# A two-block network on one core: 352 dense tokens for 384, and five stretches re-arranged

## The chip, the core and the metric

The kernel runs on one core of a Trainium2 chip. PE (TensorE) multiplies matrices, DVE (VectorE), ACT (ScalarE) and POOL (GpSimd) work on tiles, SP issues loads. The metric is the device time of one execution in microseconds (us); the lower, the better.

## What is computed

512 tokens of width 1024 pass two blocks. The first mixes them (a state-space scan and long convolutions, the "hyena" part), adds the result and applies PEER, a layer of 16384 experts:

```python
def block(hb):                                   # 128 tokens
    q = (hb @ wq).reshape(128, 8, 2, 128)
    s = einsum('thsd,snd->thsn', q, subkeys)
    s1, i1 = top_k(s[:, :, 0], 16); s2, i2 = top_k(s[:, :, 1], 16)
    cand = (s1[..., :, None] + s2[..., None, :]).reshape(128, 8, 256)
    sc, ci = top_k(cand, 16)
    idx = e1 * 128 + e2                          # from i1, i2 at ci
    gate = softmax(sc)
    act = gelu(einsum('td,thkd->thk', hb, u_tab[idx])) * gate
    return einsum('thk,thkd->td', act, v_tab[idx])
```

The second block has two layers of SwiGLU, mixers and layer norms (`x = layer_norm(alpha * x + 0.5 * ffn(x))` and the like). All is in float32.

## The kernel before

The whole program is one list of instructions for each engine, written out in Python; semaphores (`S.on`, `S.at`) tie the engines. Nothing is scheduled by a planner: the order on an engine is the order of the calls. Functions end in the engine's letter (`_t` PE, `_v` DVE, `_a` ACT, `_g` POOL, `_s` SP).

A weight block of 128 x 1024 (a "unit") is loaded by SP into one of three staging buffers, ACT rounds it to a high half (L236), and DVE or POOL subtracts to get the low half (L242; `lo_of` says which). Three pairs of halves are held. `group` (L273 to L275) makes each product from three matmuls, high by high, high by low, low by high.

PEER treats the tokens in two ways. The last NT = 384 tokens are "dense": for each of 128 chunks of 128 experts, 8 x 3 matmuls of 128 x 384 give the products with the u table ("early"), ACT's gelu follows, the result ("act") is stored to memory, multiplied later with a dense gate table, split into halves, and 128 further units of 24 matmuls ("vexp") multiply it with the v table. The first 128 tokens, one to a partition, are served by gathers: POOL issues an indirect DMA (L2047) that fetches 128 rows of 4 KB, one for each token, into one of six row buffers; 128 gathers of u rows, each multiplied and summed by DVE (L2061), then 128 of v rows, each scaled and added by DVE (L2072). A gather waits until the row six before is used. `L.steps` spreads the rows over the stages.

The stages, in order: A, the top-k search (DVE) beside 76 early chunks; B, the gates, built by DVE as one-hot tiles (L2364: one comparison; L2366: eight small ones with the gate multiplied in) and by PE's small matmuls (L2337) for four tokens at each of 96 steps, beside 38 early chunks; C, the last 14 early chunks, where ACT begins to load acts and gates back; V, 128 units of v. In A and B POOL makes the low halves of u, in V DVE makes those of v (L242) and POOL those of the acts (L292).

Ahead of PEER stand the conv stage (L832 starts a cumulative sum in PSUM banks 4 and 5), the states stage (L603 multiplies out three "modulation" rows, all in bank 6), and the long convolutions, whose filters PE makes (L1579) and DVE multiplies with a decay out of PSUM (L1597). Behind it, `back_t` ends each part of the second block: eight groups of PE, then a layer norm (L378 POOL, L405, L412, L428 PE).

## Time and profile before

| | us |
|---|---|
| median of 3 runs | 4386.53 (4385.96 to 4389.57) |
| the profiled execution | 4381.67 |
| its span | 4379.9 |
| PE busy | 4206.7 (96%) |
| DVE, ACT, POOL busy | 2993.5, 1805.0, 1425.4 |
| stages A, B, C, V | 334, 241, 61, 533 |

Busy time says how full an engine is over the whole span, and the stages differ: what a change in a stage is worth is read from the stage's own row. PE's granted clock over the execution is 0.975.

### The profile page before, as it was taken

Reading aid. Unit: us, or ns where it says so; the run is one execution under the profiler, and the core shown is the slowest. Engines: PE = TensorE matmul, PEld = TensorE weight load, DVE = VectorE, ACT = ScalarE, POOL = GpSimd, SP = SyncE. Lnnn points to the kernel's source line nnn. Section 1 sums busy time; section 2 is a strip of 40 time slices with the busy share of each in tenths; the row PEclk is TensorE's granted clock in tenths of the full one; section 3 lists DMA queues with packets and bytes.
Section 4 is the critical chain, followed back from the end, with each engine's and each line's share of the span. In section 5 each row is a group of like instructions: output and inputs, shape, how many; then the busy total and the mean of one; then the engine's idle time right before and its main releaser. Section 6 shows DMA issues by size and latency. Waiting matters only on the chain.

```text
span 4379.9 us, 66702 instructions
## 1 busy us (share of the span) xinstructions
PE 4206.7 (96%) x26175; PEld 3683.5 (84%) x26175; DVE 2993.5 (68%) x5043; ACT 1805.0 (41%) x2815; POOL 1425.4 (33%) x992
## 2 busy tenths in 40 slices
PE   7989999999999999999999999999999999999998
PEld 5756755779999999999999877799889877877997
DVE  5866667559768977777688455498388445555873
ACT  4345411233335643333355345355255333324542
POOL 2044224315886545766411210212111110112121
PEclk9989999999999999999999999899999999899999
DMA  5123521224887899999733222123323332002332
GB/s 188 63 92 127 185 69 58 90 90 149 281 267 283 332 369 364 368 373 373 263 97 106 92 79 72 61 92 97 99 92 101 101 104 92 26 36 68 107 97 77
DMA packets 232191, 665.76 MB, mean 152 GB/s; under 512 B 22519, under 2 KB 88455, under 8 KB 229704
## 3 DMA queue, kind: packets, MB, share of 16 engines
q1 hardware_dynamic: 110528, 389.87, 26.6%
...
q14 instruction: 102, 0.84, 0.1%
HBM read 593.25 MB, written 68.16 MB: 151 GB/s over the span
## 4 chain that ended last, share of the span: by engine, by line
PE 81%; DVE 10%; issue 3%; ACT 3%; POOL 2%; DMA 1%; ACTq 0%; DVEq 0%; POOLq 0%
PE ps L273 15%; PE ps L275 15%; PE ps L274 15%; PE ps L2743 5%; PE ps L2745 5%; PE ps L2744 5%; PE ps L1624 2%; PE ps L2337 2%; PE ps L3778 1%; PE ps L1703 1%; DVE A L912 1%; DVE r L292 1%; DVE r L242 1%; DMA A<-in_w_late 1%; PE ps L405 1%
## 5 line engine op out<-in xcount | busy, mean ns | idle before, releaser
L273 PE MATMUL ps<-r,r 128*128 128x384 f32 (+1 forms) x3944 | 1435.8, 364 | 14.8 <-POOL r L242 7.2
L274 PE MATMUL ps<-r,r 128*128 128x384 f32 (+1 forms) x3944 | 1418.8, 360 | 0.0
L275 PE MATMUL ps<-r,r 128*128 128x384 f32 (+1 forms) x3944 | 1418.3, 360 | 0.0
L236 ACT ACTIVATE r<-A 128x1024 fp32r<-128x1024 f32 x513 | 542.0, 1058 | 1132.7 <-PE ps L275 996.8
L242 DVE TENSOR_TENSOR r<-A,r 128x1024 fp32r<-128x1024 f32 x401 | 509.0, 1271 | 728.2 <-ACT r L236 715.9
L273 PEld LDWEIGHTS ps<-r,r 128*128 128x128 f32 x3944 | 743.0, 188 | 101.0 <-issue 13.6
L274 PEld LDWEIGHTS ps<-r,r 128*128 128x128 f32 x3944 | 743.0, 188 | 74.6 <-issue 3.6
L275 PEld LDWEIGHTS ps<-r,r 128*128 128x128 f32 x3944 | 742.2, 188 | 74.1
L289 ACT ACTIVATE r<-A 128x512 fp32r<-128x512 f32 (+1 forms) x796 | 474.1, 611 | 497.9 <-DVE A L2429 227.9
L2743 PE MATMUL ps<-r,r 128*128 128x256 f32 x2128 | 603.0, 283 | 3.4 <-DVE A L2907 2.6
L2744 PE MATMUL ps<-r,r 128*128 128x256 f32 x2128 | 602.2, 283 | 0.0
L2745 PE MATMUL ps<-r,r 128*128 128x256 f32 x2128 | 602.2, 283 | 0.0
L292 POOL TENSOR_TENSOR r<-A,r 128x384 fp32r<-128x384 f32 (+2 forms) x243 | 338.7, 1401 | 605.3 <-ACT r L289 472.6
L292 DVE TENSOR_TENSOR r<-A,r 128x512 fp32r<-128x512 f32 x617 | 449.1, 743 | 8.2 <-ACT r L289 4.4
L2743 PEld LDWEIGHTS ps<-r,r 128*128 128x128 f32 x2128 | 408.5, 192 | 5.2 <-DVE A L2907 3.4
L2744 PEld LDWEIGHTS ps<-r,r 128*128 128x128 f32 x2128 | 408.5, 192 | 0.2
L2745 PEld LDWEIGHTS ps<-r,r 128*128 128x128 f32 x2128 | 408.5, 192 | 0.0
L242 POOL TENSOR_TENSOR r<-A,r 128x1024 fp32r<-128x1024 f32 x112 | 284.2, 2539 | 231.7 <-ACT r L236 230.4
L2925 POOL TENSOR_TENSOR A<-A 128x512 f32<-128x512 f32 x72 | 121.2, 1683 | 696.9 <-DVE A L2916 696.9
L2995 DVE TENSOR_TENSOR A<-A 128x512 f32<-128x512 f32 x304 | 208.5, 686 | 3.1 <-issue 0.2
L2072 DVE SCALAR_TENSOR_TENSOR A<-A 128x1024 f32<-128x1024 f32 x127 | 173.6, 1367 | 2.1
L2047 POOL DMA_INDIRECT A<-in_v_rows,A x128 | 160.8, 1256 | 22.0 <-DVE r L242 5.8
...
## 6 DMA issues: line engine op xcount, KB each, us to landing
A<-in_pu SPq DMA_DIRECT2D x128, 512.0 KB
A<-in_pv SPq DMA_DIRECT2D x128, 512.0 KB
...
acts<-A ACTq DMA_DIRECT2D x128, 192.0 KB
...
```

The costliest lines, as they stand in the source:

```text
L236: a.activation(self.vr(self.wr0 + 2048 * (u % RW), 1024), self.v(self.st0 + 1024 * (u % RS), 1024), ACT.Copy).then_inc(*self.S.on("a", "hi ...
L242: e.tensor_tensor(self.vr(at + 1024, 1024), self.v(self.st0 + 1024 * (u % RS), 1024), self.vr(at, 1024).bitcast(F32), ALU.subtract).then_i ...
L273: t.matmul(o, hi, xh, start=first and k == k0, stop=False)
L274: t.matmul(o, hi, xl, start=False, stop=False)
L275: m = t.matmul(o, lo, xh, start=False, stop=final and k == K - 1)
L289: a.activation(self.vr(at, n), src, ACT.Copy).then_inc(*self.S.on("a", *key))
L292: e.tensor_tensor(self.vr(lo, n), src, self.vr(at, n).bitcast(F32), ALU.subtract).then_inc(*self.S.on(who, *key))
L2072: v.scalar_tensor_tensor(out=acc, in0=row, scalar=w, in1=acc, op0=ALU.mult, op1=ALU.add).then_inc(*S.on("v", "row used", n))
L2743: t.matmul(ps[:, 0:256], hi, xh, start=opens and k == 0, stop=False, skip_group_check=not opens)
L2744: t.matmul(ps[:, 0:256], hi, xl, start=False, stop=False, skip_group_check=not opens)
L2745: m = t.matmul(ps[:, 0:256], lo, xh, start=False, stop=k == 3, skip_group_check=not opens)
L2995: v.tensor_tensor(self.operand(i, p, x), self.v(one, 512), self.v(two, 512), how).then_inc(*S.on("v", "sum", i, p, x))
```

## The change

Five things are done together.

1. NT goes from 384 to 352. The 32 tokens more (NG = 160 now) are gathered too: 160 gathers of u rows and 160 of v. Gathers n of 128 to 159 hold 32 tokens times four choices in their 128 partitions; PE copies those tokens' x four times ("x again"), four small DMAs move their indices and gates ("moved"), a second accumulator takes them, and matmuls with a "fold" matrix sum the four. Gates are made in 88 steps for 96. The rows stand in other places: 64 of u in A (48 before), 76 in B (55), 17 in C (14), the rest and the v rows in V.
2. The last 14 acts stay in SBUF: they are neither stored nor loaded back. Loads of acts and gates are issued one step earlier.
3. In every second batch of one-hot tiles, DVE makes one comparison of 1024 for eight small instructions, and POOL multiplies the gate in (`hot_g`). POOL also makes the low halves of the last eight query units and the first three u units.
4. The long convolutions' filters are copied out of PSUM by ACT; of eight multiplies DVE keeps six, from SBUF, and POOL takes two (all eight on DVE before).
5. The cumulative sums go to banks 2 and 3 and no longer wait for "tok" 10; the second modulation row goes to bank 5; two weight splits of DVE move from the end of the long convolutions to the peer norm, behind its reciprocal; in the layer norms behind eight-unit groups, group 7 is issued whole, ahead of the norm's matmuls, and four filling matmuls (L435, now L436) follow.

Line numbers of the changed kernel are 1 to some 100 higher.

```diff
-UT, NT, LATER = 76, 384, 14
+UT, NT, LATER = 76, 352, 14
+NG, TG = 512 - NT, NT // 8
...
-        self.lo_of = ["g" if wq + RW < u <= wq + 128 - LATER or u == 16 else "v" for u in range(len(self.units))]
+        self.lo_of = ["g" if wq + RW - 11 < u <= wq + 128 - LATER or u == 16 else "v" for u in range(len(self.units))]
...
         v.reciprocal(r, var).then_inc(*S.on("v", "rstd", tag))
+        self.weights_v(v, units)
...
             if o == 14:
                 t.wait_ge(*S.at("aa"))
-                t.wait_ge(*S.at("tok", 10))
...
-                        m = t.matmul(PS[4][:, at:at + 16], self.cst(tri), self.v(L.AA + at, 16), start=True, stop=True)
+                        m = t.matmul(PS[2][:, at:at + 16], self.cst(tri), self.v(L.AA + at, 16), start=True, stop=True)
...
             for k in range(3 * n, 3 * n + 3) if n < 8 else ():
-                if k in (8, 16):
-                    t.wait_ge(*S.at("modrow", 3 + k // 8))
-                self.modmm_t(t, 4 + k // 8, 6, range(k % 8, k % 8 + 1))
+                if k == 16:
+                    t.wait_ge(*S.at("modrow", 4))
+                self.modmm_t(t, 4 + k // 8, (6, 5, 6)[k // 8], range(k % 8, k % 8 + 1))
...
+    def filter_direct(self, r, i):
+        return r == 0 and i % 2 == 0
+
+    def filters_a(self, a, r):
+        S = self.S
+        if r:
+            a.wait_ge(*S.at("ks", r - 1, 1, 3))
+        for i in range(8):
+            if self.filter_direct(r, i):
+                continue
+            a.wait_ge(*S.at("fil", r, i))
+            a.activation(self.filter_out(i)[0], self.ps("fil", r, i)[:, :], ACT.Copy).then_inc(*S.on("a", "out", "fil", r, i))
+
+    def filters_g(self, g, r):
+        S = self.S
+        g.wait_ge(*S.at("filter decay", r))
+        for i in self.FILTER_G:
+            h, dec = self.filter_out(i)
+            g.wait_ge(*S.at("out", "fil", r, i))
+            g.tensor_tensor(h, h, dec, ALU.mult).then_inc(*S.on("g"))
+        S.mark("g", "filter half", r)
...
-                v.wait_ge(*S.at("fil", r, i))
-                v.tensor_tensor(self.v(L.HF + 2048 * j + 512 * nt, 512), self.ps("fil", r, i)[:, :], self.v(L.DEC + 512 * nt, 512), ALU.mult).then_inc(*S.on("v", "out", "fil", r, i))
+                h, dec = self.filter_out(i)
+                if self.filter_direct(r, i):
+                    v.wait_ge(*S.at("fil", r, i))
+                    v.tensor_tensor(h, self.ps("fil", r, i)[:, :], dec, ALU.mult).then_inc(*S.on("v", "out", "fil", r, i))
+                else:
+                    v.wait_ge(*S.at("out", "fil", r, i))
+                    v.tensor_tensor(h, h, dec, ALU.mult).then_inc(*S.on("v"))
...
-        self.weights_v(v, 16)
...
-        for at, m in ([(("choices", i), 16 * (i + 1) // 3) for i in range(9)] + [(("gates", i), 48 + 55 * (i + 1) // 96) for i in range(96)]
-                      + [(("later", r), 103 + r + 1) for r in range(LATER)]
-                      + [(("second", x), min(117 + x + 1, 128) if x < 11 else 128 + min(128, 128 * (x - 10) // 108)) for x in range(128)]):
+        for at, m in ([(("choices", i), 64 * (i + 1) // 27) for i in range(27)] + [(("gates", i), 64 + 76 * (i + 1) // (NT // 4)) for i in range(NT // 4)]
+                      + [(("later", r), 140 + 17 * (r + 1) // LATER) for r in range(LATER)]
+                      + [(("second", x), min(157 + x + 1, NG) if x < 5 else NG + min(NG, NG * (x - 4) // 117)) for x in range(128)]):
...
+        if n == 128:
+            g.wait_ge(*S.at("moved"))
...
+    def act_at(self, c):
+        L = self.L3
+        if c < 128 - LATER or c >= 124:
+            return L.SP + NT * (c % 4)
+        i = c - 128 + LATER
+        return L.KEPT + NT * i if i < 7 else self.HX + 2816 + NT * (i - 7)
+
     def spill(self, a, c):
         S, L = self.S, self.L3
-        if c >= 0:
+        if 0 <= c < 128 - LATER:
             a.wait_ge(*S.at("out", "early", c))
             a.dma_start(self.acts[c], self.v(L.SP + NT * (c % 4), NT)).then_inc(*S.dma(f"sp{c % 4}", "spill", c))
 
...
         self.spill(a, c - 1)
         self.weights_a(a, 8)
         a.wait_ge(*S.at("early", c))
-        if c >= 4:
+        if c >= 124:
+            a.wait_ge(*S.at("spill", 127 - LATER - (127 - LATER - c) % 4))
...
+        a.activation(self.v(self.act_at(c), NT), self.ps("early", c)[:, 0:NT], ACT.Gelu).then_inc(*S.on("a", "out", "early", c))
...
-    ROWS = {14 + 17 * n // 16: n for n in range(48)}
+    ROWS = {c: [n for n in range(64) if 14 + 7 * n // 8 == c] for c in range(UT)}
...
+                ps = self.bank_t(t, "x again", i)
+                for q in range(4):
+                    x = self.v(L.SC0 + 512 * (4 * i + q) + 128, NG - 128)
+                    for c in range(4):
+                        m = t.matmul(ps[32 * c:32 * c + 32, 128 * q:128 * q + 128], x, self.cst("ident"), start=True, stop=True)
+                m.then_inc(*S.on("t", "x again", i))
...
+                if tt == 1:
+                    a.wait_ge(*S.at("chosen again"))
+                    for q in range(4):
+                        a.dma_start(self.A[32 * q:32 * q + 32, L.GATE:L.GATE + 2 * NG].rearrange("p (s c) -> p s c", s=2)[:, :, 128:NG],
+                                    self.A[0:32, L.EX:L.EX + 256].rearrange("p (s c) -> p s c", s=2)[:, :, 32 * q:32 * q + 32]).then_inc(*S.dma("moved"))
+                    S.mark("moved", "moved")
...
+            if b % 2 == 0:
+                v.tensor_tensor(a, io, e1.unsqueeze(2).to_broadcast([128, 8, 128]), ALU.is_equal).then_inc(*S.on("v", "one hot 1", b))
+                return
...
+    def hot_g(self, g, b):
+        S = self.S
+        if b < NT // 8 and b % 2 == 0:
+            a, h, e1, e2, gate = self.one_hot(b)
+            g.wait_ge(*S.at("one hot 1", b))
+            g.tensor_tensor(a, a, gate.unsqueeze(2).to_broadcast([128, 8, 128]), ALU.mult).then_inc(*S.on("g", "one hot gated", b))
...
-    FIRST = 6
+    FIRST = 5
...
-        elif slot % 4 == 0 and 1 <= slot // 4 < 32:
-            self.gate_load(a, slot // 4)
-        if 0 <= slot - 3 < 128:
-            self.act_load(a, slot - 3)
+        if slot % 4 == 3 and slot // 4 + 1 < 32:
+            self.gate_load(a, slot // 4 + 1)
+        if 0 <= slot - 2 < 128 - LATER:
+            self.act_load(a, slot - 2)
...
+        if k0:
+            self.group(t, [ps[:, :]], [rhs], k0, "back", i, 7, "first part", final=False)
+            self.norm_seven_t(t, tag, wk, self.LN, True)
+        else:
+            self.group(t, [ps[:, :]], [rhs], K, "back", i, 7)
+            self.warm_t(t, 0 if i in (1, 4) else 2, 4)
+            self.norm_seven_t(t, tag, wk, self.LN, True)
```

On POOL, in the middle of stage B, before (L2047 gathers, L242 low halves, r the weight buffers):

```order
L2047 DMA A<-in_u_rows,A 128x1024 x2
L242 TENSOR_TENSOR r_51<-A,r_50 128x1024
L2047 DMA A<-in_u_rows,A 128x1024
L242 TENSOR_TENSOR r_55<-A,r_54 128x1024
L2047 DMA A<-in_u_rows,A 128x1024 x2
L242 TENSOR_TENSOR r_87<-A,r_86 128x1024
L2047 DMA A<-in_u_rows,A 128x1024
L242 TENSOR_TENSOR r_51<-A,r_50 128x1024
L2047 DMA A<-in_u_rows,A 128x1024 x2
L242 TENSOR_TENSOR r_55<-A,r_54 128x1024
```

and now (L2091 gathers, L243 low halves, L2460 the gate multiply):

```order
L2091 DMA A<-in_u_rows,A 128x1024 x2
L243 TENSOR_TENSOR r_51<-A,r_50 128x1024
L2091 DMA A<-in_u_rows,A 128x1024
L2460 TENSOR_TENSOR A<-A 128x1024
L2091 DMA A<-in_u_rows,A 128x1024
L243 TENSOR_TENSOR r_55<-A,r_54 128x1024
L2091 DMA A<-in_u_rows,A 128x1024 x2
L2460 TENSOR_TENSOR A<-A 128x1024
L243 TENSOR_TENSOR r_87<-A,r_86 128x1024
L2091 DMA A<-in_u_rows,A 128x1024 x2
L243 TENSOR_TENSOR r_51<-A,r_50 128x1024
L2091 DMA A<-in_u_rows,A 128x1024 x2
```

The gate multiplies stand between the gathers and low halves, and two gathers stand where there was one.

On DVE, in the second of the four filter rounds, before (L1597 is the filter's multiply, L1655 and L1659 products with spectra):

```order
L1655 TENSOR_TENSOR A<-ps,A 128x512
L1597 TENSOR_TENSOR A<-ps,A 128x512 x3
L1655 TENSOR_TENSOR A<-ps,A 128x512 x2
L1659 TENSOR_TENSOR A<-A 128x512
L1655 TENSOR_TENSOR A<-ps,A 128x512 x2
L1597 TENSOR_TENSOR A<-ps,A 128x512 x3
L1655 TENSOR_TENSOR A<-ps,A 128x512
L1659 TENSOR_TENSOR A<-A 128x512
L1655 TENSOR_TENSOR A<-ps,A 128x512 x3
L1659 TENSOR_TENSOR A<-A 128x512
L1597 TENSOR_TENSOR A<-ps,A 128x512 x2
L1601 TENSOR_TENSOR A<-A 1x512
```

and now (the multiply is L1633, the products L1692 and L1696):

```order
L1692 TENSOR_TENSOR A<-ps,A 128x512
L1633 TENSOR_TENSOR A<-A 128x512 x3
L1692 TENSOR_TENSOR A<-ps,A 128x512 x2
L1696 TENSOR_TENSOR A<-A 128x512
L1692 TENSOR_TENSOR A<-ps,A 128x512 x2
L1633 TENSOR_TENSOR A<-A 128x512 x2
L1692 TENSOR_TENSOR A<-ps,A 128x512
L1696 TENSOR_TENSOR A<-A 128x512
L1692 TENSOR_TENSOR A<-ps,A 128x512 x3
L1696 TENSOR_TENSOR A<-A 128x512
L1633 TENSOR_TENSOR A<-A 128x512
L1637 TENSOR_TENSOR A<-A 1x512
```

The multiply reads SBUF (A) where it read PSUM (ps), and two of eight are gone.

On PE, at the end of the group behind the first mixer, before (L273 to L275 the group's last unit, L412 and L405 the norm, L435 a filling matmul):

```order
L275 MATMUL ps<-r_126,r_51 128x512
L412 MATMUL ps<-A 128x512
L405 MATMUL ps<-A 128x1 x8
L273 MATMUL ps<-r_127,r_50 128x512
L274 MATMUL ps<-r_102,r_50 128x512
L275 MATMUL ps<-r_127,r_51 128x512
L435 MATMUL ps<-A 128x512
L405 MATMUL ps<-A 128x1 x8
L425 MATMUL ps<-A 128x512
L428 MATMUL ps<-A 128x128 x4
```

and now (L276 ends the group, L436 fills, L413 and L406 are the norm):

```order
L274 MATMUL ps<-r_127,r_50 128x512
L275 MATMUL ps<-r_102,r_50 128x512
L276 MATMUL ps<-r_127,r_51 128x512
L436 MATMUL ps<-A 128x512 x4
L413 MATMUL ps<-A 128x512
L406 MATMUL ps<-A 128x1 x16
L426 MATMUL ps<-A 128x512
L429 MATMUL ps<-A 128x128 x4
L436 MATMUL ps<-A 128x512 x2
```

The unit's three matmuls stood behind the norm's first matmuls and stand ahead of them now.

## Rows read from the trace of the kernel before

**Rows 1.** The page's first line and the chain of waits by engine.
```profile
span 4379.9 us, 66702 instructions
...
PE 81%; DVE 10%; issue 3%; ACT 3%; POOL 2%; DMA 1%; ACTq 0%; DVEq 0%; POOLq 0%
```

**Rows 2.** Windows by stage: length, busy us (instructions) by engine, clock, DMA share, GB/s.
```profile
850.00:890.00 40.00, 40.00 (x176) 32.81 (x175) 11.95 (x13) 11.96 (x14) 6.48 (x5) 1.00 0.46 145
1013.00:1347.00 334.00, 326.75 (x1885) 325.00 (x1884) 254.62 (x607) 127.01 (x175) 259.44 (x124) 0.99 0.73 240
1347.00:1588.00 241.00, 241.00 (x1657) 241.00 (x1656) 227.64 (x511) 145.86 (x169) 141.75 (x96) 1.00 0.90 334
1588.00:1649.00 61.00, 59.23 (x341) 58.59 (x340) 42.86 (x53) 24.85 (x38) 22.66 (x20) 1.00 1.03 389
1740.00:2182.00 442.00, 442.00 (x2555) 441.84 (x2553) 332.25 (x334) 167.17 (x211) 289.24 (x217) 1.00 0.96 350
2250.00:2350.00 100.00, 100.00 (x835) 100.00 (x835) 87.66 (x161) 52.02 (x99) 16.84 (x10) 1.00 0.34 105
```

**Rows 3.** Lines of GpSimd in stage A: busy, mean ns, idle before and releasers.
```profile
L242 POOL TENSOR_TENSOR r<-A,r 128x1024 fp32r<-128x1024 f32 x76 | 197.9, 2605 | 138.9 <-ACT r L236 137.6 <-issue 0.3
L2047 POOL DMA_INDIRECT A<-in_u_rows,A x48 | 62.6, 1304 | 27.2 <-DVE A L2061 20.6 <-issue 4.6 <-DVE A L2257 0.5
```

**Rows 4.** Lines in 1194.5 to 1197.5 us, a stretch of stage A.
```profile
L2267 DVE TENSOR_TENSOR A<-A 128x2048 f32<-128x2048 f32 x1 | 5.0, 5026 | 0.1
L2047 POOL DMA_INDIRECT A<-in_u_rows,A x1 | 2.8, 2823 | 0.2 <-issue 0.2
```

**Rows 5.** Lines in stage B.
```profile
L2366 DVE TENSOR_SCALAR A<-ps,A 128x128 f32<-128x128 f32 x357 | 118.0, 410 | 0.0
...
L242 POOL TENSOR_TENSOR r<-A,r 128x1024 fp32r<-128x1024 f32 x36 | 86.4, 2400 | 80.8 <-ACT r L236 80.8
...
L2047 POOL DMA_INDIRECT A<-in_u_rows,A x60 | 56.7, 946 | 19.2 <-DVE A L2061 7.5 <-issue 6.0 <-DVE A L2366 2.8
...
L2364 DVE TENSOR_TENSOR A<-ps,A 128x1024 f32<-128x1024 f32 x44 | 54.0, 1227 | 0.0
```

**Rows 6.** Lines in stage V.
```profile
L2072 DVE SCALAR_TENSOR_TENSOR A<-A 128x1024 f32<-128x1024 f32 x127 | 173.6, 1367 | 2.1
L292 POOL TENSOR_TENSOR r<-A,r 128x384 fp32r<-128x384 f32 x121 | 166.3, 1375 | 143.6 <-ACT r L289 143.4
L2047 POOL DMA_INDIRECT A<-in_v_rows,A x128 | 160.8, 1256 | 22.0 <-DVE r L242 5.8 <-issue 4.9
L242 DVE TENSOR_TENSOR r<-A,r 128x1024 fp32r<-128x1024 f32 x127 | 157.6, 1241 | 132.3 <-ACT r L236 123.4 <-issue 8.9
...
L2429 DVE TENSOR_TENSOR A<-A 128x384 f32<-128x384 f32 x120 | 66.8, 557 | 1.2 <-DMA A<-acts 1.1
```

**Rows 7.** DMA of 1590 to 1650 us (stage C), then of 1740 to 2100.
```profile
DMA packets 10977, 23.45 MB, mean 391 GB/s; under 512 B 819, under 2 KB 7685, under 8 KB 10854
...
DMA packets 62565, 133.74 MB, mean 372 GB/s; under 512 B 4754, under 2 KB 38348, under 8 KB 62540
```

**Rows 8.** Waits at 186 to 260 us: engine, line, releaser, total, times, longest.
```profile
PE ps L832 <- DVE A L876: 5.5, 1, 5.5
...
PE ps L603 <- DVE A L624: 6.0, 2, 4.5
...
DVE A L1042 <- PE ps L1007: 8.1, 2, 4.8
```

**Rows 9.** Lines in 510 to 760 us (long convolutions).
```profile
L1579 PE MATMUL ps<-A 64*128 64x512 f32 x64 | 25.2, 721 | 12.9 <-DVE A L1597 12.9
...
L1597 DVE TENSOR_TENSOR A<-ps,A 128x512 f32<-128x512 f32 x32 | 20.3, 681 | 1.1 <-PE ps L1579 1.0
```

**Rows 10.** Waits of PE at 898 to 912 us, then at 2785 to 2830.
```profile
PE ps L428 <- DVE A L466: 3.2, 1, 3.2
...
PE ps L412 <- POOL A L378: 3.0, 1, 3.0
```

More of the change, by code:

```diff
@@ L442, in off_four_v, with norm_apply_v @@
             v.scalar_tensor_tensor(out=self.H(k), in0=self.PS[b][:, :], scalar=-1.0 / 512, in1=self.H(k), op0=ALU.mult, op1=ALU.add).then_inc(*S.on("v", "off four", tag, k))
-    def norm_apply_v(self, v, tag, last, dsts, gains, eps, banks, mean, parts):
+    def norm_apply_v(self, v, tag, last, dsts, gains, eps, banks, mean, parts, units=0):
         S = self.S
@@ L1546, in load_filter @@
             a.wait_ge(*S.at("filter", r - 1))
+            a.wait_ge(*S.at("filter half", r - 1))
         for i, x in enumerate((L.a, L.b)):
@@ L1614, in spectrum_t @@
             t.wait_ge(*S.at("filter", r))
+            t.wait_ge(*S.at("filter half", r))
         else:
@@ L1823, in long_s @@
         s.wait_ge(*S.at("filter", 3))
+        s.wait_ge(*S.at("filter half", 3))
         s.wait_ge(*S.at("scan kept"))
@@ L2000, in lay_peer @@
         L.XT, L.ROWS, L.ACC = self.al(1024), self.al(6144), self.al(1024)
-        L.DOT, L.COEF, L.GATE, L.IDX = (self.al(128) for _ in range(4))
+        L.DOT, L.COEF, L.GATE, L.IDX = (self.al(NG) for _ in range(4))
         L.SP = self.al(4 * NT)
@@ L2056, in rows_v @@
         for n in L.steps[at]:
-            row, c = self.v(L.ROWS + 1024 * (n % 6), 1024), n % 128
+            row, c = self.v(L.ROWS + 1024 * (n % 6), 1024), n % NG
+            if n == 128:
+                v.wait_ge(*S.at("out", "x again", 1))
             v.wait_ge(*S.at("row", n))
-            if n < 128:
-                tokens = self.last2[:, :] if n < L.kept else self.v(L.XT, 1024)
+            if n < NG:
+                tokens = self.last2[:, :] if c < 128 else self.v(L.XT, 1024)
                 v.scalar_tensor_tensor(out=row, in0=row, scalar=1.0, in1=tokens, op0=ALU.mult, op1=ALU.mult,
@@ L2075, in rows_a @@
         S, L = self.S, self.L3
-        if L.steps[at] and L.steps[at][-1] == 127:
-            a.wait_ge(*S.at("row used", 127))
-            a.activation(self.v(L.COEF, 128), self.v(L.DOT, 128), ACT.Gelu).then_inc(*S.on("a", "row acts"))
+        if L.steps[at] and NG - 1 in L.steps[at]:
+            a.wait_ge(*S.at("row used", NG - 1))
+            a.activation(self.v(L.COEF, NG), self.v(L.DOT, NG), ACT.Gelu).then_inc(*S.on("a", "row acts"))
     def topk_s(self, s):
@@ L2176, in topk_a @@
             self.weights_a(a, 8)
[L2177 to L2180 removed]
+            if o in (3, 4):
+                i = o - 3
+                a.wait_ge(*S.at("x again", i))
+                a.activation(self.v(L.XT + 512 * i, 512), self.ps("x again", i)[:, :], ACT.Copy).then_inc(*S.on("a", "out", "x again", i))
             a.wait_ge(*S.at("q", o))
@@ L2218, in best_v @@
             v.max(v8(i, 1), part(alt, i)).then_inc(*S.on("v", "max 2", what, tt, i))
+        if rows is not None:
+            self.rows_v(v, "choices", rows + 2)
         for i in range(n):
@@ L2227, in topk_v @@
         self.after(v, "v", "first")
-        self.norm_apply_v(v, "peer", None, [self.v(L.SC0 + 512 * k, 512) for k in range(8)], [self.col(2, k) for k in range(8)], 1e-6, self.L2.norm, False, L.HN)
+        self.norm_apply_v(v, "peer", None, [self.v(L.SC0 + 512 * k, 512) for k in range(8)], [self.col(2, k) for k in range(8)], 1e-6, self.L2.norm, False, L.HN, 16)
         i16u, ciu, cju = self.v(L.I16, 128).bitcast(U32), self.v(L.CI, 128).bitcast(U32), self.v(L.CJ, 256).bitcast(U32)
@@ L2242, in topk_v @@
             v.wait_ge(*S.at("x tokens", i))
-            v.wait_ge(*S.at("out", "x tokens", i))
         v.wait_ge(*S.at("residual kept", "peer"))
@@ L2300, in topk_g @@
             self.weights_g(g, 8)
-            if c in self.ROWS:
-                if self.ROWS[c] == 0:
+            for n in self.ROWS[c]:
+                if n == 0:
                     g.wait_ge(*S.at("chosen"))
-                    g.wait_ge(*S.at("out", "x tokens", 1))
-                self.gather(g, self.ROWS[c])
+                    g.wait_ge(*S.at("out", "x again", 1))
+                self.gather(g, n)
     def gates_early(self, i):
@@ L2383, in gates_g @@
         S, L = self.S, self.L3
-        for n in range(48, 52):
+        self.hot_g(g, 0)
+        for n in range(64, 68):
             self.gather(g, n)
         for i in range(NT // 4):
+            if i % 2 == 0:
+                self.hot_g(g, i // 2 + 2)
             if self.gates_early(i) is not None:
@@ L2424, in prepare_v @@
             n = c // 4
-            ac = self.v(L.TM + NT * (c % 8), NT).rearrange("p (g t) -> p g t", g=8)
-            v.wait_ge(*S.at("act back", c))
+            ac = self.act_parts(c)[0].rearrange("p (g t) -> p g t", g=8)
+            v.wait_ge(*(S.at("act back", c) if c < 128 - LATER else S.at("out", "early", c)))
             if c % 4 == 0:
@@ L2466, in tables_t @@
             if x == 6:
-                t.wait_ge(*S.at("row used", L.kept - 1))
+                t.wait_ge(*S.at("row used", 127))
             if x == 125:
-                t.wait_ge(*S.at("row used", 255))
-                for i in range(2):
+                t.wait_ge(*S.at("row used", 2 * NG - 1))
+                for i in range(3):
                     sm = self.bank_t(t, "sum t", i)
-                    for q in range(4):
-                        m = self.tr(t, sm[:, 128 * q:128 * q + 128], self.v(L.ACC + 512 * i + 128 * q, 128))
+                    for k in range(3 * i, min(3 * i + 3, 8)):
+                        at = NG * (k % 3)
+                        self.tr(t, sm[:, at:at + 128], self.v(L.ACC + 128 * k, 128))
+                        m = t.matmul(sm[:, at + 128:at + NG], self.v(L.XT + 128 * k, 128), self.cst("fold"), start=True, stop=True)
                     m.then_inc(*S.on("t", "sum t", i))
```

117 lines of the change are left out of this document (68 added, 49 removed).

## The prediction

> **What bounds the kernel now.** I read the page first. The span is 4379.9 us, and the chain of waits gives PE 81% of it and DVE 10% [rows 1]. So the question in each stage is whether PE waits, and then what its instructions cost. The windows by stage answer that [rows 2]. In stage A (search and first dense products, 1013 to 1347) PE is busy 326.75 of 334 us; in B (gates, 1347 to 1588) 241 of 241; in C (1588 to 1649) 59.23 of 61; in V (the products with the v rows, the part after 1740 taken) 442 of 442. These 1170 us are what the change rewrites. Around them stand the small waits of the first half and of the layer norms, which I read in the waits of PE and DVE.
>
> The second thing to see is how full the others are. DMA moves 334 GB/s in B, 389 in C, and its engines are busy 0.90 to 1.03 there and 0.96 in V. DVE is busy 227.64 of 241 in B.
>
> **A dense matmul.** Start to start it takes 442/2555 = 173.0 ns at 384 columns, 100/835 = 119.8 at 256, 40/176 = 227.3 at 512 [rows 2], all at granted clock 1.00 (the 2.4 GHz level). That is a straight line, 0.42 ns a column, so 352 columns take 159.7 ns. A unit of 24 goes from 4.152 to 3.832 us, a saving of 0.32; 76 units in A, 38 in B, 14 in C, 128 in V. The gates have 88 steps for 96: B's 241 us less 912 x 173.0 ns leaves 83.2 us for 745 gate matmuls, 112 ns each, and 64 fewer save 7.2. If PE set every stage the saving would be 24.3 + 19.4 + 4.5 + 41.0 = 89 us. But 32 tokens move to gathered rows: 32 u gathers and 32 v gathers more, half a MB each, and each stage must be asked whether GpSimd, DVE and DMA hold the new pace.
>
> **Stage A.** GpSimd makes the low halves (2.605 us) and issues the gathers (1.304 mean) in one queue [rows 3]. With 64 gathers over 56 units, one unit asks it for 2.605 + 64/56 x 1.304 + 0.1 of issue (4.6 us over 48 gathers) = 4.20 us, more than PE's 3.83. So 56 units x 4.20 = 235, 20 units x 3.83 = 77, and some 6 of the 11 us of other matmuls (326.75 - 76 x 4.152) beside them: 318 for 334, gain 16. The gather has two prices in the trace, about 0.95 [rows 5] and 2.823 while DVE ran a 2048-element operation of 5.026 us [rows 4]. All at 0.946 would leave PE the bound (gain 24, and 31 with the waits gone); with some more at 2.8 the gain falls to 5.
>
> The rows sit in 27 slots between DVE's steps for 9, so GpSimd's 20.6 us of waits for used rows [rows 3] should shrink; what is late next is GpSimd's own work, as counted. The eleven low halves moved to GpSimd before A lie where its queue is empty, and cost nothing; back on DVE they would be 11 x 1.24.
>
> **Stage B.** PE needs 241 - 12.2 - 7.2 = 221.6 us. GpSimd gets 36 low halves at 2.400, 80 gathers (60 before) at 0.946 and 22 gate multiplies; such a multiply is not in the trace, its nearest row is the low half of the same size, so 2.40 (bounds 1.4, by the row lo of 384 elements [rows 6], and 2.6): 86 + 76 + 53 = 215 us, and 251 with A's means. I take 232, between them and nearer neither. Each even multiply also makes PE wait for GpSimd, and behind it in that queue stand gathers which wait for rows that DVE frees (7.5 + 2.8 us before [rows 5]). DVE loses 22 groups of eight small multiplies (118.0/357 x 8 = 2.64 us) for one comparison of 1.227, and 4 batches of 3.87, and gains 22 rows of 1.3: 228 - 31 - 15 + 29 = 210, so 0.95 of PE's time. DMA moves 334 GB/s x 241 = 80.5 MB, plus 21 gathers less shorter gates and acts: 89 MB, 228 us at C's 391 GB/s [rows 7]. So three resources stand at 0.95 to 1.05 of PE: 234 us, gain 7, from 0 to 19.
>
> **Stage C.** Fourteen stores go, gathers go from 14 to 17, loads come one step earlier: 23.45 MB become about 22.7, 58 us at 391 GB/s, where PE needs 54. PE's waits are 1.8 now. Gain 2, from 0 to 6.
>
> **Stage V.** Per unit DMA brings a v block (0.524 MB), an act and a gate part (0.180 each, 0.197 before) and 160/117 gathered rows (0.717; 128/108 before, 0.621): 1.602 MB for 1.539. Before, 1.539 in 4.152 us is 371 GB/s, and the trace has 372 [rows 7]: PE set that pace, not DMA, since PE never waited. What DMA can do is shown only by C, 391 over 60 us. At that rate a unit takes 4.10 us, over PE's 3.83. This holds for the units 5 to 101; after that no act is left to load (1.42 MB, 3.63 us) and PE sets 3.83, as before unit 5. Gain 97 x 0.055 + 31 x 0.32 = 5.3 + 9.9 = 15. If C's rate isn't the limit, 41; if 372 is, 97 x 4.31 and a loss of 5. DVE there needs 160/117 x 1.367 + 1.241 + 0.55 = 3.66 us per unit, GpSimd 160/117 x 1.256 + 1.375 = 3.09 [rows 6]: both under 3.83.
>
> The Trainium skill speaks against this gain: "DMA: Bandwidth & Descriptors", Specifications, gives a core about 358 GB/s from memory and 368 as the vendor's derated figure. By 368, V's unit would be 4.35 us, longer than before. V's 372 fits that rule, C's 391 doesn't, so here the measured 391 decides.
>
> **The small edits.** The cumulative sums no longer wait for the turned tokens: PE stood 5.5 us there [rows 8]; gain 5.5, from 0 to 8. The second modulation row gets its own bank: PE waited 6.0 for its reader, DVE 8.1 for PE [rows 8], partly the same time; gain 6, from 0 to 8. The filters: PE's matmuls waited 12.9 us for DVE's 32 multiplies of 681 ns out of PSUM [rows 9]. ScalarE now empties the banks; of the multiplies 24 stay on DVE. Gain 13, bounds 5 (a quarter of DVE's 20.3) and 20 (all of it). Late next there are GpSimd's two multiplies, before which the spectrum can't start. The peer norm's DVE work before its scaling loses two splits of 1.24: PE waited 3.2 [rows 10]; gain 1.5, from 0 to 2.5. In the two norms behind K = 8 the last group no longer stands behind PE's wait for GpSimd (3.0 in the one shown [rows 10], and 2.5 in the other): gain 5, from 0 to 7. Against that stand 32 small matmuls for the copied tokens and 16 for the sum: 2 us by 40 to 60 ns each, an estimate below the 112 ns above. Together 5.5 + 6 + 13 + 1.5 + 5 - 2 = 29 us, from 8 to 42.
>
> **Sum.** 16 + 7 + 2 + 15 + 29 = 69. The profiled execution took 4381.67 us, so 4312.7; the median of the runs, 4386.53, stands 4.9 above it, so 4317.5.
>
> **Rivals.** (1) PE sets every stage: neither DMA nor GpSimd is at its end. For it: no wait in B and V, gathers of 0.95 in B. Against it: GpSimd's 4.20 in A. 89 + 29 = 118, 4268.
>
> (2) DMA stops at 372 GB/s: V loses 5, C 2, B gains 1, A 16: 10 + 29 = 39, 4347. For it: DMA busy 0.96 in V already. Against it: C's 391.
>
> (3) The stages go as forecast but the small waits only move, each to the next late engine (GpSimd's filter multiplies, the norms' own chain): 40 + 4, 4342. Against it: PE there waits for one releaser each, and that one is gone.
>
> (4) Slower: GpSimd's gathers are slowed by DVE in B as well as in A, and PE now waits for GpSimd's gate multiply behind them. If half of the 80 gathers take 2.82 (mean 1.89), GpSimd needs 86 + 53 + 151 + 8 = 298 us in B, 57 more than the stage has now; A gains nothing, and V, C and the small edits give 46: 4397. It decides against the kernel from a mean gather of 1.75. For it: the 2.823 row beside DVE's long operation, and rows that DVE multiplies now have both inputs in SBUF for the last 32. Against it: the mean of 0.946 in B with DVE busy 0.94.
>
> The Trainium skill has a rule for (4): "SBUF — State Buffer", SBUF: two separate sides, says that DVE and GpSimd share a port pair as an exclusive lock, taken by two-input operations of DVE. By it the 12 late rows of B and the multiplies would block one another, which A's row agrees with; B's 0.946 shows it doesn't bite there yet.
>
> **How the numbers follow.** Forecast 0.52, (1) 0.16, (2) 0.17, (3) 0.11, (4) 0.04. The forecast's own range is 4295 to 4340. The whole range, to hold 8 in 10, reaches to (1) and past (2): 4268 to 4354. A difference below 0.2% (8.8 us) can't be told from none. Faster holds for all but (4) and a little of the tail of (2) and (3): 0.94; same 0.03; slower 0.03.
>
> **What would show it.** Matmuls in V start 160 ns apart when they run. In V PE should wait 0.2 to 0.3 us per unit, for the high or low halves or acts behind a late load, up to about unit 101 and not after; DMA near 390 GB/s. If PE never waits there, (1); if DMA stays at 370, (2). In A the low halves on GpSimd should be what PE waits for, at about 4.2 us per unit. In B GpSimd should be busy over 0.9, gathers near 0.95. The waits of PE at the cumulative sums, the modulation row and the filters should be gone. I am wrong if B takes over 245 us, if V's unit is over 4.2, or if the stages outside A to V give under 15 us.

## The result, and the profile after

The changed kernel takes 4345.64 us (median of 3 runs, 4344.54 to 4354.75) against 4386.53: the ratio is 0.9918, 95% interval 0.9891 to 0.9946, 0.8% faster. The forecast was 4317. The time lies in the upper part of the whole range, 4268 to 4354, and outside the forecast's own, 4295 to 4340; 41 us were gained where 69 were forecast. The profiled execution is the slowest of the three, 4354.75 us, 27 less than the profiled one of before, so the table below shows a smaller gain than the medians do.

The page of the changed kernel, first line and chain by engine, answers to [rows 1]:

```profile
span 4352.9 us, 66771 instructions
...
PE 59%; DVE 16%; DMA 8%; issue 6%; POOL 5%; ACT 5%; ACTq 1%; DVEq 0%; POOLq 0%
```

PE's share of the chain falls from 81% to 59%. The windows by stage (length, busy time of PE, its weight loads, DVE, ACT, POOL, granted clock, DMA share, GB/s) of A, B, C, the middle of V and its end answer to [rows 2]:

```profile
1007.00:1340.00 333.00, 306.28 (x1887) 300.69 (x1887) 279.83 (x632) 126.06 (x176) 283.04 (x147) 0.98 0.80 266
1340.00:1569.00 229.00, 223.94 (x1593) 223.19 (x1593) 210.58 (x368) 140.51 (x162) 198.36 (x130) 0.99 0.97 369
1569.00:1636.00 67.00, 56.88 (x338) 56.01 (x337) 49.03 (x62) 24.69 (x39) 35.70 (x26) 0.95 0.97 367
1720.00:2050.00 330.00, 316.10 (x1925) 310.48 (x1924) 293.30 (x271) 117.01 (x161) 279.51 (x191) 0.98 1.03 390
2050.00:2157.00 107.00, 104.30 (x644) 102.23 (x642) 89.14 (x88) 38.14 (x51) 72.35 (x50) 0.98 0.86 313
```

PE now waits in every stage: 27 us in A, 5 in B, 10 in C, 14 and 3 in V. POOL is busy 0.85 in A where it was 0.78, DVE 0.89 in V, DMA moves 390 GB/s there. PE's granted clock is lower too, 0.95 to 0.99 where it was 0.99 to 1.00. The part of the clock that was not granted, times the length, sums to 21 us over these windows and to 3 over A, B, C and V before [rows 2]: an estimate, from these rows, of up to 18 us that the lower clock cost.

The stages by the starts of their first dense matmuls, in us:

| stretch | before | after | measured | forecast |
|---|---|---|---|---|
| start to the first filter matmul | 565.3 | 549.0 | -16.3 | -11.5 |
| long convolutions, to the last inverse matmul | 244.3 | 252.0 | +7.7 | -13 |
| from there to A | 203.5 | 206.1 | +2.6 | +0.5 |
| A | 333.8 | 332.5 | -1.3 | -16 |
| B | 241.2 | 229.1 | -12.1 | -7 |
| C | 60.5 | 66.9 | +6.4 | -2 |
| V | 533.7 | 520.9 | -12.8 | -15 |
| behind PEER | 2197.7 | 2196.4 | -1.3 | -5 |

The sum is -27, as the two spans have it. Two rows carry most of the miss, the long convolutions (21 us) and A (15), then C (8). A second profile of the changed kernel (its repeat among the experiments) gives 546.5, 255.7, 204.5, 330.6, 228.8, 66.9, 526.8 and 2184.3 us for the rows: V and the stretch behind PEER differ by 6 and 12 us between two executions of one kernel, the other rows by at most 4.

### The profile page after: what moved, and what is told of

Read it like the earlier page. It is cut to its first block, busy times and chain, and to the rows that moved or that the text cites. A ratio compares the mean times of both kernels' runs of the same rounds, so it can differ in the third digit from the quotient of the medians.

```text
span 4352.9 us, 66771 instructions
## 1 busy us (share of the span) xinstructions
PE 4132.9 (95%) x26203; PEld 3596.0 (83%) x26203; DVE 3064.4 (70%) x4933; ACT 1794.7 (41%) x2835; POOL 1632.6 (38%) x1097
## 4 chain that ended last, share of the span: by engine, by line
PE 59%; DVE 16%; DMA 8%; issue 6%; POOL 5%; ACT 5%; ACTq 1%; DVEq 0%; POOLq 0%
PE ps L274 9%; PE ps L276 9%; PE ps L275 9%; PE ps L2846 5%; PE ps L2848 5%; PE ps L2847 5%; DMA A<-in_u_rows,A 2%; DMA A<-in_v_rows,A 2%; ACT r L237 2%; POOL r L243 2%; DVE A L2120 2%; DVE r L243 2%; PE ps L3881 2%; DVE A L913 1%; POOL A L2091 1%
## 5 line engine op out<-in xcount | busy, mean ns | idle before, releaser
L274 PE MATMUL ps<-r,r 128*128 128x352 f32 (+1 forms) x3944 | 1421.9, 361 | 53.2 <-POOL r L243 20.5
L275 PE MATMUL ps<-r,r 128*128 128x352 f32 (+1 forms) x3944 | 1398.1, 354 | 0.0
L276 PE MATMUL ps<-r,r 128*128 128x352 f32 (+1 forms) x3944 | 1398.0, 354 | 0.0
L243 DVE TENSOR_TENSOR r<-A,r 128x1024 fp32r<-128x1024 f32 x390 | 522.9, 1343 | 617.8 <-ACT r L237 617.3
L275 PEld LDWEIGHTS ps<-r,r 128*128 128x128 f32 x3944 | 748.4, 190 | 75.0 <-issue 3.6
L276 PEld LDWEIGHTS ps<-r,r 128*128 128x128 f32 x3944 | 746.8, 189 | 74.7
L293 POOL TENSOR_TENSOR r<-A,r 128x352 fp32r<-128x352 f32 (+2 forms) x243 | 330.5, 1367 | 500.3 <-ACT r L290 374.9
L243 POOL TENSOR_TENSOR r<-A,r 128x1024 fp32r<-128x1024 f32 x123 | 304.0, 2472 | 121.8 <-ACT r L237 120.2
L2091 POOL DMA_INDIRECT A<-in_v_rows,A x160 | 252.0, 1575 | 30.8 <-issue 11.8
L2120 DVE SCALAR_TENSOR_TENSOR A<-A 128x1024 f32<-128x1024 f32 x158 | 218.4, 1382 | 24.1 <-DMA A<-in_v_rows,A 20.7
```

Of the source, the lines that this page charges most:

```text
L243: e.tensor_tensor(self.vr(at + 1024, 1024), self.v(self.st0 + 1024 * (u % RS), 1024), self.vr(at, 1024).bitcast(F32), ALU.subtract).then_i ...
L274: t.matmul(o, hi, xh, start=first and k == k0, stop=False)
L275: t.matmul(o, hi, xl, start=False, stop=False)
L276: m = t.matmul(o, lo, xh, start=False, stop=final and k == K - 1)
L293: e.tensor_tensor(self.vr(lo, n), src, self.vr(at, n).bitcast(F32), ALU.subtract).then_inc(*self.S.on(who, *key))
L2091: g.indirect_dma_start(self.v(L.ROWS + 1024 * (n % 6), 1024), None, self.T["u_rows" if n < NG else "v_rows"], bass.IndirectOffsetOnAxis(in ...
```

## The experiments

Each is an edit of the changed kernel. Whole times of one kernel spread by 15 to 32 us here (4326.0 to 4357.6 in the first experiment), and four of the runs (short rows in C, A without gathers, all gates on DVE, the old banks) have one execution each, so most verdicts rest on a stage's time in the profile. The runs with short rows and the one without gathers leave out bytes or rows that the result needs; they serve to read a stage only.

**The filters.** All eight multiplies on DVE out of PSUM:

```diff
-    FILTER_G = (5, 7)
+    FILTER_G = ()
-        return r == 0 and i % 2 == 0
+        return True
```

> The changed kernel with the filters as before: all eight multiplies of a round on DVE out of PSUM, no copies on ACT, none on GpSimd. Theory 1 (a DVE multiply whose two inputs lie in SBUF takes 0.68 us alone and up to 1.76 beside a GpSimd multiply, so the copied filters cost the long convolutions more than the bank waits gave): the stretch from the first filter matmul to the last inverse group goes from 233.8 us back to the 223.7 of the kernel before, and the time from 4345.6 to about 4336. Rival (the filters' edit gains as forecast, and the loss there has another cause): the stretch gets 5 to 13 us longer, 4351 to 4358.

The long convolutions took 242.2 us by the table's marks (252.0 in the changed kernel, 244.3 before), 10 less. The expectation measured between other marks, and the difference is the same. The time was 4338.9 us, within the spread. Theory 1 holds. DVE's lines in the convolutions, of the changed kernel (545 to 745 us):

```profile
L1633 DVE TENSOR_TENSOR A<-A 128x512 f32<-128x512 f32 x20 | 24.2, 1243 | 1.8 <-ACT A L1607 1.8
...
L1637 DVE TENSOR_TENSOR A<-A 1x512 f32<-1x512 f32 x4 | 6.7, 1670 | 0.1
```

and of this run (495 to 735 us):

```profile
L1630 DVE TENSOR_TENSOR A<-ps,A 128x512 f32<-128x512 f32 x32 | 20.1, 679 | 1.4 <-PE ps L1581 1.4
...
L1637 DVE TENSOR_TENSOR A<-A 1x512 f32<-1x512 f32 x4 | 2.7, 680 | 0.1
```

PE's waits in the long convolutions of the changed kernel (545 to 801 us), the largest, and then PE's wait for the banks in this run (495 to 735 us):

```profile
PE ps L1661 <- DVE A L1696: 8.8, 4, 4.8
PE ps L1661 <- DVE A L1787: 6.9, 2, 3.4
PE ps L1740 <- DVE A L1696: 5.4, 3, 2.7
PE ps L1661 <- DVE A L1639: 4.5, 2, 3.1
...
PE ps L1581 <- DVE A L1630: 2.6, 1, 2.6
```

```profile
PE ps L1581 <- DVE A L1630: 12.9, 6, 3.2
```

Twenty multiplies from SBUF cost DVE 24.2 us, thirty-two from PSUM 20.1; a multiply of one row takes 1.67 us for 0.68. And the 12.9 us that the edit was to save are back to the last digit, while the stage is 10 us shorter. With the copied filters the wait for the banks had fallen to 2.6 us, but PE waited longer for what DVE does after its multiplies (L1696, L1787, L1639): 33.2 us in all, against 21.8 in this run and 21.4 before. The wait had moved and grown. The timeline of the changed kernel shows the price being paid:

```profile
590.08 2.94 POOL L1712 TENSOR_TENSOR A<-A 128x512 f32<-128x512 f32 x2 [1.23 <-DVE A L1692]
590.52 3.05 DVE L1633 TENSOR_TENSOR A<-A 128x512 f32<-128x512 f32 x2
```

Two multiplies of DVE and two of POOL run side by side, and take 3.05 and 2.94 us; DVE's two would be 1.36 at the price out of PSUM [rows 9]. The Trainium skill states this in "SBUF — State Buffer", Who interferes with whom: a DVE instruction with two SBUF inputs contends with a GpSimd instruction that reads SBUF, and one with at most one SBUF input, outside the 2-port perf modes, does not. For the multiplies the trace agrees with both halves, 1.243 against 0.679 us. The one-row copy behind them (L1639), with one SBUF input, also grew, from 0.415 us in this run to 1.131 in the changed kernel; whether it is in such a mode no run here shows.

Copying only the two tiles that GpSimd multiplies:

```diff
-        return r == 0 and i % 2 == 0
+        return i not in self.FILTER_G
```

> The changed kernel with ACT copying only the two filter tiles that GpSimd multiplies; DVE takes the other six from PSUM. Theory 1: DVE's multiplies are 0.68 us again, PE waits for banks less than before since two tiles leave DVE, but the two one-row operations beside GpSimd's multiplies stay long (1.6 us): the stretch takes 218 to 227 us, the time 4330 to 4339. Rival (what costs is GpSimd's two multiplies at the end of each round, not DVE's inputs): the stretch stays at 231 to 234 us, 4343 to 4346.

245.3 us: most of the 10 us come back with DVE's inputs alone, so the rival falls. PE's wait for the banks is 12.9 us again, and not less as expected; all its waits in the stretch sum to 22.1 us, as in the run before (21.8). The one-row multiply averages 0.952 us, less than the 1.6 expected. So the last 3 us are not a wait of PE: its granted clock was 0.91 over the stretch here and 0.93 in the run before, by estimate 5 us of 245. The whole time, 4342.4 us, lies between the two ranges expected.

**Stage C.** The loads in their old places:

```diff
-        if slot % 4 == 3 and slot // 4 + 1 < 32:
-            self.gate_load(a, slot // 4 + 1)
-        if 0 <= slot - 2 < 128 - LATER:
+        elif slot % 4 == 0 and 1 <= slot // 4 < 32:
+            self.gate_load(a, slot // 4)
+        if 0 <= slot - 3 < 128 - LATER:
-    FIRST = 5
+    FIRST = 6
```

> The changed kernel with act and gate loads issued in the old places (one gate load at a time, acts one step later). Theory 2 (two gate loads issued together fill ACT's queue, the next issue stands 9.3 us, and PE waits 4.55 us for ACT behind it): stage C takes 61 to 63 us for the 67 of the changed kernel's profile, the time about 4341. Rival (stage C is at the DMA's limit and ACT's stall only shows it): stage C stays at 65 to 68 us, the time within 2 us of 4345.6.

C took 67.7 us, and the whole time was 4353.8 us, 8 above the changed kernel's where the rival expected 2 at most; that is within the spread. My theory 2 falls: the long issue on ACT's queue is a symptom. These are rows of ACT's timeline in C of the changed kernel (ACTq is its issuing of DMAs):

```profile
1582.82 1.06 ACT L237 ACTIVATE r<-A 128x1024 fp32r<-128x1024 f32 x1 [8.65 <-DMA A<-in_pu]
...
1591.20 9.31 ACTq L2504 DMA_DIRECT2D A<-acts  x1
1600.61 1.06 ACT L237 ACTIVATE r<-A 128x1024 fp32r<-128x1024 f32 x1 [9.18 <-issue]
```

ACT waits 8.65 us for a u block and then stands 9.31 us in the issue of one load; PE waited 4.02 and 4.55 us behind them:

```profile
1584.28 0.50 PE L274 MATMUL ps<-r,r 128*128 128x352 f32 x1 [4.02 <-ACT A L2166]
...
1602.07 0.66 PE L274 MATMUL ps<-r,r 128*128 128x352 f32 x1 [4.55 <-ACT A L2166]
```

With the old loads the same two came, 8.39 and 7.60. So I asked whether bytes or order delay them, with fewer bytes and the same instructions:

```diff
+        wide = 256 if 138 <= n < 160 else 1024
-        g.indirect_dma_start(self.v(L.ROWS + 1024 * (n % 6), 1024), None, self.T["u_rows" if n < NG else "v_rows"],
+        g.indirect_dma_start(self.v(L.ROWS + 1024 * (n % 6), wide), None, self.T["u_rows" if n < NG else "v_rows"].rearrange("e (f x) -> (e f) x", x=wide),
```

> The changed kernel with gathers 138 to 159 (the last of B and all of C) fetching 256 columns for 1024: 8.7 MB left out, no instruction and no wait. Theory 4 (C is late because more bytes are asked for in it than DMA brings, the gathered rows among them): C falls from 67 us to 58 to 61. Rival (C is late by the order in which the transfers stand: u blocks behind the last store of gates, and ACT behind its own full queue): C stays at 64 to 68.

C fell to 58.9 us, and PE's waits for ACT in it from 10.1 us to 3.6: bytes. But V took 532.2 us for 520.9, so C and V together took 591 for 588. Why V was slower in this run is open: in ten other profiles with V's bytes unchanged it was 517 to 527, and C and V together 585 to 597, so this run doesn't show whether the 8 us would be kept.

**Stages A and V.** The same edit on the gathers of A and on most v rows, `wide = 256 if 6 <= n < 64 or 166 <= n < 320 else 1024`:

> The changed kernel with gathers 6 to 63 (all in stage A) and 166 to 319 (nearly all v rows, in stage V) fetching 256 columns for 1024: three quarters of their bytes are left out, every instruction and wait stays. Theory 3 (V is bound by DMA at 390 GB/s, A by GpSimd's queue of low halves and gathers): V's unit falls from 4.07 to 3.81 to 3.85 us, the stage from 521 to about 492; stage A stays within 6 us of 332. Rival for A (late u blocks and rows set it): A falls by 15 us or more, to under 318. Rival for V (DVE or GpSimd set it): V stays over 510.

V fell to 502.3 us, 3.90 a unit for 4.07 between units 5 and 101, and A stayed at 331.4. So the bytes are the larger part of V's excess over 3.83, and not all of it; they don't set A. In V of the changed kernel (1636 to 2050 us) PE waits for DVE's low halves, and DVE for gathered rows:

```profile
PE ps L274 <- DVE r L243: 13.6, 10, 4.7
...
DVE A L2120 <- DMA A<-in_v_rows,A: 15.7, 13, 2.5
```

The middle of V in the run with short rows, and what PE's weight loads still wait for in it (1650 to 2040 us):

```profile
1720.00:2040.00 320.00, 318.55 (x1966) 313.81 (x1964) 300.04 (x274) 117.38 (x162) 287.06 (x193) 1.00 0.82 270
```

```profile
PEld ps L274 <- DVE r L243: 5.4, 15, 0.6
```

At 270 GB/s PE is busy all but 1.5 us and its granted clock is 1.00 for 0.98, which is a part of the gain. Its matmuls are still 320/1966 = 162.8 ns apart for 160. DVE, busy 0.94, is the next one: the 5.4 us that the weight loads wait for its low halves are 0.05 us a unit, most of what lies between 3.83 and 3.90.

A without the gathers 6 to 63:

```diff
-        if n >= 2 * NG:
+        if n >= 2 * NG or 6 <= n < 64:
             return
-            v.wait_ge(*S.at("row", n))
+            v.wait_ge(*S.at("row used", n - 6) if 6 <= n < 64 else S.at("row", n))
```

> The changed kernel without the gathers 6 to 63, the ones of stage A (GpSimd doesn't issue them, nothing is fetched; DVE still does its instruction on each row). Theory 3 (GpSimd's one queue of low halves and gathers, 4.18 us per unit, sets A, and its order, not the bytes): A falls from 332 us to 298 to 308, PE busy nearly throughout. Rival (DVE's rows and ACT's fixed place for the exponentials hold PE up): A stays over 320.

A fell to 308.7 us, just over the expected 308. PE's wait for the low halves of GpSimd, first in the changed kernel (1063 to 1340 us), then in this run (1063 to 1317 us):

```profile
PE ps L274 <- POOL r L243: 20.5, 18, 2.7
```

```profile
PE ps L274 <- POOL r L243: 3.2, 2, 2.1
```

GpSimd's queue is what sets A. Its lines in 1063 to 1340 us of the changed kernel, which answer to [rows 3]:

```profile
L243 POOL TENSOR_TENSOR r<-A,r 128x1024 fp32r<-128x1024 f32 x64 | 157.9, 2468 | 17.5 <-ACT r L237 16.4
L2091 POOL DMA_INDIRECT A<-in_u_rows,A x68 | 89.3, 1313 | 12.3 <-issue 8.3 <-DVE A L2107 0.6 <-DVE A L2332 0.5
L2460 POOL TENSOR_TENSOR A<-A 128x1024 f32<-128x1024 f32 x2 | 3.8, 1902 | 0.0
```

157.9 + 89.3 + 3.8 us busy and 29.8 idle are 280.8, the stretch of 277 and the ends of instructions that reach over its edges: GpSimd pauses for little else than ACT's high halves (16.4 us) and between issues (8.3). What ACT waits for there, and what SP's loads of u blocks wait for:

```profile
ACT r L237 <- DMA A<-in_pu: 99.7, 38, 6.3
```

```profile
SPq L217 <- POOL r L243: 250.1, 64, 8.3
```

A load of a u block starts when GpSimd's low half has freed its staging buffer. So GpSimd waits, by way of ACT and the load, for a buffer that it frees itself.

**Stage B.** All one-hot batches on DVE:

```diff
-            if b % 2 == 0:
+            if False:
-        if b < NT // 8 and b % 2 == 0:
+        if False:
```

> The changed kernel with all one-hot batches on DVE as before, none multiplied by GpSimd. If DVE would set B then (210 + 31 us of work): B takes 240 to 246 us for 229, and A ends some us sooner. Rival (DMA sets B, at 369 GB/s in it): B stays at 227 to 233.

B took 240.5 us with DVE busy 235.4, so DVE would have set it; and A took 321.9 instead of 332.5. GpSimd's part in the gates saves 11 us in B and costs 11 in A (9 against the second profile), so the two stages together took 562 us either way. At the end of A PE waits for it, here at 1300 to 1345 us of the changed kernel, and the clock falls (window of 1300 to 1340 us):

```profile
PE ps L2421 <- POOL A L2460: 5.6, 1, 5.6
```

```profile
1300.00:1340.00 40.00, 32.71 (x197) 31.87 (x196) 25.46 (x39) 16.96 (x24) 32.10 (x19) 0.91 0.75 249
```

The first gate multiply stands in GpSimd's queue, behind A's last low halves and gathers, and B's first gate matmuls wait for it. The wait is 5.6 us of the loss; in these 40 us the granted clock is 0.91, which is up to 3.6 more, where it was 1.00 over the last 40 us of A in the run without these multiplies.

**The banks.** The old banks and waits of the conv and states stages:

```diff
+                t.wait_ge(*S.at("tok", 10))
-                        m = t.matmul(PS[2][:, at:at + 16], ...
+                        m = t.matmul(PS[4][:, at:at + 16], ...
...
-                if k == 16:
-                    t.wait_ge(*S.at("modrow", 4))
+                if k in (8, 16):
+                    t.wait_ge(*S.at("modrow", 3 + k // 8))
```

> The changed kernel with the cumulative sums in banks 4 and 5 behind the wait for the turned tokens again, and the three modulation rows in one bank. If the two edits gave the 17 us that the conv and states stages are shorter: the first filter matmul starts at 565 us for 549. Rival (part of the 17 is the clock's, which was granted at 0.72 to 0.88 there before): it starts at 555 to 560.

The first filter matmul starts at 564.1 us; the two edits are worth 15, more than the waits of PE by themselves (11.5). With the old banks PE's waits are again 5.5 and 5.9 us [rows 8]. The rival falls as it was put, at 555 to 560. The granted clock from 165 to 270 us was 0.84 here and 0.87 in the changed kernel, so a part of the other 3 to 4 us may be the clock's; that isn't shown.

**A better version.** The filters as before, and GpSimd's multiplies only from batch 4 on:

```diff
-    FILTER_G = (5, 7)
+    FILTER_G = ()
-        return r == 0 and i % 2 == 0
+        return True
-            if b % 2 == 0:
+            if b % 2 == 0 and b >= 4:
-        if b < NT // 8 and b % 2 == 0:
+        if 4 <= b < NT // 8 and b % 2 == 0:
```

> The changed kernel with the filters as before, and GpSimd's gate multiplies from batch 4 on (DVE makes batches 0 to 3). Theory 1 and 5 (the copied filters cost 10 us; GpSimd's first multiplies stand ahead of the last low halves of A and hold PE 5.6 us at its end): the long convolutions take 242 us for 252, A 320 to 325 for 332, B 228 to 232; about 18 us less than the changed kernel on the same chip. Rival to 5 (A's 10 us go over to B, whose DVE is then late): A and B together stay at 559 to 563, and the gain is 10.

> The changed kernel again, as the measure for the two others on the same chip: 4340 to 4352, its stages as in its first profile within 3 us, V within 8.

It took 4333.8 us (4324.9 to 4339.7), the changed kernel on the same chip 4352.4 (4345.4 to 4359.3): 18.6 us less where 18 were expected. (The repeated kernel came out just above its expected 4340 to 4352.) The long convolutions took 243.6 us, A 323.4, B 227.8, all near what was expected. Against the kernel before, the ratios are 0.9893 (0.9875 to 0.9910) and 0.9939 (0.9923 to 0.9956). Its A and B by windows:

```profile
997.00:1320.00 323.00, 303.74 (x1880) 298.91 (x1879) 280.14 (x637) 124.71 (x175) 275.21 (x141) 1.00 0.81 270
1320.00:1548.00 228.00, 222.85 (x1596) 221.94 (x1596) 211.00 (x377) 141.67 (x162) 203.60 (x134) 1.00 0.98 377
```

A is 9 us shorter than in the first profile of the changed kernel and 7 shorter than in the second, and B as short. The same with 56 rows in A for 64, and 84 in B for 76 (`56 * (i + 1) // 27`, `56 + 84 * (i + 1) // (NT // 4)`, one row for each unit from 14 on):

> e9_both_undone with 56 u rows in stage A and 84 in B, for 64 and 76. Theory 3 (A is GpSimd's at 4.18 us per unit, of which a gather is 1.3): A falls by 8 to 10 us more, to 311 to 316. B gets 4.2 MB more: if DMA sets it (369 GB/s in it, 390 at most) it grows by up to 8; if not, by 3. Together 0 to 7 us less than e9_both_undone.

A fell by 11.6 us to 311.8, as expected; B rose by 10.2 to 238.0, more than the 8 that were the most expected; and the time is the same, 4333.8 us. Where B ends up, and PE's largest wait in it (1309 to 1547 us):

```profile
1309.00:1547.00 238.00, 226.56 (x1597) 225.16 (x1596) 220.94 (x394) 141.87 (x162) 210.23 (x141) 0.99 0.98 377
```

```profile
PE ps L2421 <- POOL A L2460: 9.2, 4, 3.0
```

B brought its 4.2 MB more at the same 377 GB/s, which would fit a bound by DMA. But that is not shown: the eight rows also gave DVE 10 us more work (211.00 to 220.94), and PE's wait for GpSimd's gate multiplies rose from 5.2 to 9.2 us. No run here took more than two rows' bytes out of B. A is GpSimd's, what sets B stays open among DMA, DVE and that queue, and a row moved between the two gains nothing.

## Why the prediction was right or wrong

*The number.* Of the 40 us forecast in A to V, 20 came, and of the 29 outside, 7. The forecast's own range was missed. The whole range held because it was drawn past rival (2). The 4347 us of (2) and the 4342 of (3) are near the measured time, but neither describes what happened, so that is partly luck. One of the prediction's signs of being wrong came up: the stages outside A to V gave under 15 us (7; 20 in the second profile, which was 12 us faster behind PEER). The bounds of that sum were also added wrongly: its terms give 3 to 43.5, and not 8 to 42.

*The clock, put at nothing.* The sums for A to V took PE's pace at granted clock 1.00, also where PE was to wait. The windows after show 0.95 to 0.99, by the estimate above up to 18 us.

*The pace of a matmul.* Right: 160.0 ns is the median distance of starts in V, 159.7 was read from the straight line through three widths.

*Stage A, off by 15.* GpSimd's price was right: 157.9 + 89.3 + 12.3 us over 62 units are 4.18 each, 4.20 forecast (the low half was shorter than assumed, 2.468 for 2.605, and the idle time between issues longer). The step that failed is the sum behind it, 56 units at this pace and the rest at PE's. It gave GpSimd no wait of its own. It waited 16.4 us for ACT, which waited for u blocks, whose buffers GpSimd frees: when the bound engine also releases the buffers, its pauses add to its work. And it left out the two gate multiplies in front of B, whose place between gathers and low halves the forecast had named for B alone; moving them back gave 7 to 11 us in A.

*Stage B, better by 5.* The gate multiply took 1.925 us for the assumed 2.40, and the gathers averaged 1.024 (lines of GpSimd in 1340 to 1569 us):

```profile
L2091 POOL DMA_INDIRECT A<-in_u_rows,A x74 | 75.8, 1024 | 20.6 <-issue 9.3 <-DVE A L2107 7.2 <-DVE A L2453 1.7
L2460 POOL TENSOR_TENSOR A<-A 128x1024 f32<-128x1024 f32 x21 | 40.4, 1925 | 6.0 <-DVE A L2450 5.8
```

GpSimd was busy 198 of 229 us, 0.87, and not over 0.9 as foreseen.

*Stage C, off by 8.* The step "gain 2" counted 22.7 MB at 391 GB/s, 58 us. DMA from 1569 to 1636 us of the changed kernel:

```profile
DMA packets 10124, 24.56 MB, mean 367 GB/s; under 512 B 746, under 2 KB 5800, under 8 KB 9993
```

Both terms were off: 1.9 MB more are 5 us, and the lower rate is 4. Eighteen gathers were issued in C for twelve before, where 17 for 14 were counted. Its bytes were the cause, as the shortened rows showed, but the two waits of 4 us could not be read from an average.

*Stage V.* Right in the main mechanism: 4.07 us per unit between units 5 and 101 where 4.10 was worked out from C's rate, at 390 GB/s. The near sum, 12.8 us for 15, is luck: these 96 units gave 8.8 us where 5.3 were forecast, the units before and after them 4 for 9.9. The end was forecast at PE's pace, 3.83, and took 111 us for 27 units, 4.1. Of the 8 us over that pace 2.7 are waits of PE and up to 2 the clock, 0.98; the rest is open. In the second profile the unit took 4.11 and V gave 7 us. Rival (1) is out, since PE waits in every stage. Rival (2), whose 4347 us is nearest to the measured time, is out as well: it reaches that time by 372 GB/s, which V exceeds (381 to 395 over 330 us in its middle in all profiles with whole rows), and the loss lies elsewhere. The Trainium skill ("DMA: Bandwidth & Descriptors", Specifications) gives a vendor's derated figure of 368 GB/s, which the prediction held against V. V's 390 over 330 us shows that it did not bind here.

*The long convolutions, off by 21.* This is the step that failed most. It read PE's 12.9 us of waits as the gain, and priced DVE's multiply from SBUF at PSUM's 0.681 us. The runs showed 1.243 us, and PE's waits in the stage at 33.2 us where they had been 21.4. The other price could have been read from the trace of before: the product L1659 has the same shape with both inputs in SBUF, and it averaged 0.980 us in 510 to 760 us (0.691 to 1.597 over the whole run):

```profile
L1659 DVE TENSOR_TENSOR A<-A 128x512 f32<-128x512 f32 x24 | 23.5, 980 | 0.8
```

The rule that the two engines block one another stood in the prediction, but only beside rival (4), for stage B. There the gathers stayed at 1.02 us, so rival (4) is out.

*The other small edits.* The banks gave 15 to 16 for 11.5. PE's wait in the peer norm fell from 3.2 us to 1.5, and the copies of the tokens took 2.2 us by themselves, where 2 were counted for all small matmuls. In the norms behind K = 8 both waits are gone and what follows starts 5 and 2 us sooner [rows 10]; the stretch behind PEER moved only 1.3 us in this profile and 13 in the second, since its clock differs from run to run (below). Rival (3), that the small waits only move, held for the filters, where they grew, and for none of the other edits.
